# Interleaving the high and low halves of the weights, value by value

## The reference, cut to what matters

```python
proj = h @ w_in[l]                                   # q, k, v of both attentions, two gates
x = x + gate1[:, None, :] * (merged @ w_out[l])
y = jnp.square(jax.nn.relu(h2 @ w_mlp_in[l])) @ w_mlp_out[l]
...
def swiglu(h, w_gate, w_up, w_down):                 # four times in the second block
    return (jax.nn.silu(h @ w_gate) * (h @ w_up)) @ w_down
...
y = jnp.einsum('blgc,gcd->blgd', pooled, w_group)    # the pooling mixer
k_nope = (c_kv @ w_uk).reshape(B, L, N_HEADS, QK_NOPE)
v = (c_kv @ w_uv).reshape(B, L, N_HEADS, V_HEAD)
```

## Time and profile before

| | before |
|---|---|
| median of 3 runs | 1234.65 us |
| the profiled execution | 1234.03 us |
| its span, first to last instruction | 1232.3 us |
| TensorE matmul busy | 1208.6 us |
| VectorE busy | 862.2 us |
| ScalarE busy | 633.9 us |
| mean granted TensorE clock | 0.998 of full speed |

### The profile page before, as it was taken

One profiled execution on the slowest core, in us unless ns is written; L12 is line 12 of the kernel. 1 busy time (PEld: TensorE's weight loads), 2 busy tenths in 40 slices (PEclk: granted clock), 3 DMA queues, 4 the chain that ended last, 5 costly groups with the idle time before them and its releaser, 6 DMA issues.

```text
span 1232.3 us, 23766 instructions
## 1 busy us (share of the span) xinstructions
PE 1208.6 (98%) x9956; PEld 1185.4 (96%) x9956; DVE 862.2 (70%) x1214; ACT 633.9 (51%) x985; POOL 172.2 (14%) x178
## 2 busy tenths in 40 slices
PE   6999999999999999999999999999999999999997
PEld 4999999999999999999999999999999988999996
DVE  6789888776756766556766656766666777766654
ACT  6557546675545444434544444454444567544541
POOL 3024323000322000012200001320001221000021
PEclk9999999999999999999999999999999999999999
DMA  9997775667564555654455565456556533555551
GB/s 361 321 338 269 240 251 172 240 235 261 168 220 154 177 172 172 204 173 136 124 185 171 172 204 173 148 180 201 177 191 200 188 120 95 203 199 177 191 164 35
DMA packets 67563, 239.17 MB, mean 194 GB/s; under 512 B 7380, under 2 KB 9573, under 8 KB 67456
## 3 DMA queue, kind: packets, MB, share of 16 engines
q1 hardware_dynamic: 66800, 235.41, 57.2%
q0 software_dynamic: 656, 2.24, 0.5%
HBM read 236.55 MB, written 1.07 MB: 193 GB/s over the span
## 4 chain that ended last, share of the span: by engine, by line
PE 93%; DVE 2%; issue 0%; ACT 0%; POOL 0%; DVEq 0%
PE G L611 28%; PE G L610 28%; PE G L612 28%; PE A L610 1%; PE A L612 1%; PE A L611 1%; DVE sb_wlo L1568 0%; PE A L762 0%; PE A L1056 0%; PE A L777 0%; PE A L750 0%; PE G L1111 0%; PE G L1112 0%; PE G L1113 0%; PE A L1090 0%; PE A L640 0%
## 5 line engine op out<-in xcount | busy, mean ns | idle before, releaser
L1568 DVE TENSOR_TENSOR sb_wlo<-sb_raw,sb_whi 128x1024 fp32r<-128x1024 f32 (+1 forms) x398 | 487.9, 1258 | 77.4 <-ACT sb_whi L1169 77.3
L610 PE MATMUL G<-sb_xh,sb_whi 128*128 128x256 f32 (+2 forms) x1752 | 496.5, 283 | 0.4 <-DVE sb_wlo L1568 0.4
L611 PE MATMUL G<-sb_xl,sb_whi 128*128 128x256 f32 (+2 forms) x1752 | 496.8, 284 | 0.0
L612 PE MATMUL G<-sb_xh,sb_wlo 128*128 128x256 f32 (+2 forms) x1752 | 495.1, 283 | 0.0
L1169 ACT ACTIVATE sb_whi<-sb_raw 128x1024 fp32r<-128x1024 f32 (+1 forms) x397 | 404.5, 1045 | 175.5 <-PE G L612 156.9
L610 PEld LDWEIGHTS G<-sb_xh,sb_whi 128*128 128x128 f32 x1752 | 329.7, 188 | 0.9 <-DVE sb_wlo L1568 0.7
L612 PEld LDWEIGHTS G<-sb_xh,sb_wlo 128*128 128x128 f32 x1752 | 329.3, 188 | 0.0
L611 PEld LDWEIGHTS G<-sb_xl,sb_whi 128*128 128x128 f32 x1752 | 329.2, 188 | 0.0
L610 PE MATMUL G<-sb_hh,sb_whi 128*128 128x256 f32 (+1 forms) x1056 | 296.0, 280 | 1.5 <-DVE sb_hh L1809 1.4
L612 PE MATMUL G<-sb_hh,sb_wlo 128*128 128x256 f32 (+1 forms) x1056 | 296.1, 280 | 0.0
L611 PE MATMUL G<-sb_hl,sb_whi 128*128 128x256 f32 (+1 forms) x992 | 279.0, 281 | 0.0
(11 more groups left out here) (335 smaller groups left out, 1225.2 us busy)
## 6 DMA issues: line engine op xcount, KB each, us to landing
sb_raw<-in_wstream SPq DMA_DIRECT2D x438, 512.0 KB, 4.4
sb_raw<-in_wstream SPq DMA_DIRECT2D x8, 320.0 KB, 7.6
sb_bias<-bias_scratch POOLq DMA_DIRECT2D x1, 2048.0 KB, 16.8
sb_X<-in_xT SPq DMA_DIRECT2D x2, 512.0 KB, 5.1
out_T<-sb_X SPq DMA_DIRECT2D x4, 256.0 KB, 2.7
sb_con<-in_consts SPq DMA_DIRECT2D x1, 601.0 KB, 10.1
sb_band<-in_bands SPq DMA_DIRECT2D x1, 314.0 KB, 5.1
sb_vec<-in_vecs SPq DMA_DIRECT2D x1, 82.5 KB, 2.0
```

Source lines behind the costliest of these rows:

```text
L610: e.matmul(out, w_h, xs, start=k0 + s.kt == 0, stop=False)
L611: e.matmul(out, w_h, xr, start=False, stop=False)
L612: m = e.matmul(out, w_l, xs, start=False, stop=k0 + s.kt == ktotal - 1)
L1568: e.tensor_tensor(wlo[:, i % NSPLIT, 0:w], raw[:, c % NRAW, 0:w], f(whi[:, i % NSPLIT, 0:w]), ALU.subtract).then_inc(lo_done, 1)
```

## The change

One buffer takes the place of two. Its last axis holds the high and the low half of one weight value side by side. `whi` and `wlo` become views of it, so every instruction that writes or reads a half, on any engine, goes through memory with a step of two values (8 bytes) where it had a step of one (4 bytes). The number of bytes in the buffers is the same (2 x 20 KB in each partition), and so is every instruction, wait and loop.

```diff
         raw = sb("raw", [P, NRAW, CH * P])
-        whi, wlo = sb("whi", [P, NSPLIT, CH * P], F32R), sb("wlo", [P, NSPLIT, CH * P], F32R)
+        halves = sb("halves", [P, NSPLIT, CH * P, 2], F32R)
+        whi, wlo = halves[:, :, :, 0], halves[:, :, :, 1]
         vec = sb("vec", [P, vn])
```

## The result

| | before | after |
|---|---|---|
| median | 1234.68 us | 1285.17 us (1284.79 to 1286.01, 4 runs) |
| ratio after / before | | 1.0412, 95% interval 1.0394 to 1.0430 |
| span of the profiled execution | 1232.3 us | 1283.3 us |
| TensorE / VectorE / ScalarE busy | 1208.6 / 862.2 / 633.9 us | 1260.6 / 862.8 / 673.4 us |

The kernel became slower, as forecast, but by 50.5 us where 24 were forecast. Half of the loss is the predicted one, the weights that stream as the moving operand. The other half comes from the stationary loads, for which the prediction counted nothing.

A forecast was written before the change was run, and what follows sets the result against it. The prediction took TensorE, busy for 98% of the span, as the bound. Its terms, 0 + 24 + 0 + 0 us for loads, moving reads, ScalarE's writes and VectorE's splits, took 1234.03 to 1258 us; range 1232 to 1350.

The forecast's parts named there:

- (b): TensorE's moving reads, 58,368 columns: stepped, they slow by 0.39 ns a column; taken 24 us, bounds 0 and 45 us.
- (a): TensorE's 9288 stationary loads: a step of two costs nothing, by the walking rate; taken 0, bounds 0 and 873 us.
- rival 2: Stationary load slows and becomes TensorE's bound: 2131 us in full, 1314 if loads lose 10%; chance 0.15, a third under 1350.
- (c): ScalarE's stepped writes of halves: taken 0; bound 314 us on an engine with 598 us idle.
- (d): VectorE's low splits, stepped reading and writing: taken 0, bound 0.79 us each; its one cast counted 0, uncovered 0.6 us.
- rival 3: Elementwise low splits slow and VectorE becomes the bound: 1350 us with moving reads; chance 0.12.
- Rival 1: A step of two costs nothing anywhere, even for the moving stream: 1234 us; chance 0.28.

The follow-up runs named there:

- loads only: Changed kernel, but chunks whose weights move (value projection, pooling mixer, uv) hold high and low halves apart; the others stay interleaved: 1259.17 us, 1.0196 of before.
- writes stepped: Against the changed kernel, ScalarE and VectorE still access halves at a step of two, TensorE reads without a step: 1235.10 us, 1.0000 of before.

## Why the prediction was half right

- **(b), moving reads, 24 us.** Right in place and size: 25 us measured alone (1.0203), and the pace that was named for it: 0.27 and 0.43 to 0.45 us expected, 0.284 and 0.4565 found. Its argument, that the stream can't walk twice as far as the rows show, gave the right number but isn't the mechanism: a step of three or four walks further and costs the same. And the rows that it took its 0.83 ns a column from have nothing to do with a step: they are matmuls at the lower clock. The clock record of before begins only at 19.4 us, and the 1.00 that the earlier trace rows show for 16.4 to 19.1 us is not measured. In "loads only" the record begins earlier, and the same matmuls, 0.213 us apart there too, run at a granted clock of 0.5. That this pace lay near the 0.89 ns of a stepped stream was luck. The window:

```profile
15.90:19.30 3.40, 3.35 (x15) 3.35 (x16) 3.02 (x3) 2.58 (x3) 3.25 (x3) 0.50 1.04 413
```

- **(a), stationary loads, taken at 0.** This is the step that failed: 24 us measured alone (1.0196, and 1.0197 with plain writes). The term was to be read from a margin. The prediction had the pieces, 0.112 us a load and a stream of 0.113 to 0.117, and said in rival 2 that a load slower by more than 4% shows at once. It then ruled this out because the *moving* operand walks 1024 bytes in 112 to 117 ns. That rate was as coarse as the margin it had to decide on, and it was the other operand's: a load with a step turned out at 0.118 us alone and 0.120 within a gemm. The margin was misread as well. The 5 ns come from the stretch in the earlier trace rows; in the MLP output, where matmuls started 0.113 us apart, there were 2. TensorE's 9956 matmuls stand in the same order in the traces before and after, so each distance can be set beside its own. Behind stationary loads they grew by 21.6 us in sum at 256 columns (5256 loads, 4.1 ns each: 6.7 in the MLP output, 4.7 from 1092 us on, 0.4 in the query and key gemm), 1.0 us at 258 (768 loads) and 2.6 us at 272 (3264 loads); at the moving reads by 25.3 us.
- **(c), ScalarE's writes.** The cost was taken as 0, with writes of 1051 ns as before. Each write is 10% longer, and that costs no time, by the idle time that was named as the bound's cover (writes stepped: 1.0000).
- **(d), VectorE.** 1267 to 1268 ns, as taken, and no loss on the cast. With it rival 3 falls, and so does what stood beside it: the Trainium skill, "Vector Engine (DVE) Microarchitecture Reference" (section "Measured stream behaviour on trn2"), wants two adjacent values for the full rate; a step of two with none adjacent ran at the full rate here (1268 ns against 1267), which that rule does not allow. A step of four took 2.06 us for 1024 values, 2.0 ns each, inside that page's 1.7 to 2.5 ns for a hop at every value.
- **Rival 1** (nothing costs) is out for both operands of TensorE and holds for VectorE. **Rival 2** came true in its mild form, with a chance of 0.05: 10% was priced at 56 us, 1314 with (b); it was 5%, and 24, and 1258 + 24 = 1282 is 3 us from the result. By its own rule (5 ns to spare, 9.3 us for each further ns) a load slower by 6 ns would have cost about 9 us. The rest is that loads within a gemm became 8 ns slower, not 6, and that less than 5 ns were to spare in places.

## What to carry to other kernels

When an operation is hidden by a few ns and repeated thousands of times, price the margin and not the operation: a resource with 4% of slack can't be assumed free unless the row that frees it is finer than 4%. And read a margin where it is smallest, not in one stretch. On TensorE keep both operands packed; if two tensors must share a buffer, interleave them in runs of at least four float32 values where they are the moving operand (no run loads a stationary block from such runs). A step of two float32 values cost ScalarE 10% a write and VectorE nothing; a step of four nearly doubled the time of both.

## What the runs showed that was not expected

- The moving stream at two rates only: 0.46 to 0.47 ns a value in runs of four or 16, 0.89 to 0.91 in pairs and at steps of two, three and four; the slow one is the same at a granted clock of 0.5 and of 1.0.
- The load, by 16-byte lines: about 1.84 ns a line from a step of two on, as in the table.
- Before the change, matmuls of 258 columns started 0.1195 us apart and those of 256 between 0.113 and 0.117, by the stage: two columns more for 2 to 6 ns. No run tests why.
- VectorE's cast into a step of two kept its 0.67 ns a value (682 and 684 ns), with a line touched every 1.3 ns; so the cost per line of the loads isn't one of every engine's writes.
